# Moving the output-projection partial products of an attention stage behind its last head, and taking three small VectorE steps apart

## What is computed

```python
sc = einsum('bqhcd,bkhcd->bhcqk', qb, kb) * scale        # c = 0, 1
p = softmax(where(causal, sc, NEG_INF))
a = p[:, :, 0] - lam * p[:, :, 1]
outs.append(einsum('bhqk,bkhe->bqhe', a, vb))
...
o = rms_norm(o, sub_norm) * (1.0 - lam_init)
x = x + o.reshape(b, s, N_HEADS * V_DIM) @ w_o
```

## Time and profile before

| | before |
|---|---|
| median of 3 runs | 1104.06 us |
| profiled execution | 1104.02 us, span 1102.2 us |
| TensorE busy | 1092.7 us, 99% of the span |
| VectorE busy | 785.6 us, 71% |
| ScalarE busy | 479.7 us, 44% |
| granted TensorE clock | 1.000 |

### The profile page before, as it was taken

The page is one execution under the profiler, slowest core; times in us unless marked ns, Lnnn a source line. Parts: engine busy times, 40 slices in busy tenths (PEclk is TensorE's granted clock), DMA queues, the critical chain, the costliest instruction groups (busy, mean ns, idle before and its releaser), DMA issues.

```text
span 1102.2 us, 13435 instructions
## 1 busy us (share of the span) xinstructions
PE 1092.7 (99%) x5168; PEld 901.6 (82%) x5168; DVE 785.6 (71%) x980; ACT 479.7 (44%) x695; POOL 77.3 (7%) x58
## 2 busy tenths in 40 slices
PE   8999999999999999999999999999999999999998
PEld 7888888888888888888888877778888888888887
DVE  4765554787787787788764488966678688678686
ACT  7221234354353353354632367845444344344442
POOL 0000012000000000001430122103000000000000
PEclk9999999999999999999999999999999999999999
DMA  7433463314415315301232201072313414314202
GB/s 191 101 92 101 139 204 96 112 42 156 113 39 170 98 38 172 96 1 39 96 115 96 95 24 36 2 230 77 96 58 129 120 58 141 108 58 151 79 0 77
DMA packets 144752, 105.90 MB, mean 96 GB/s; under 512 B 12592, under 2 KB 121136, under 8 KB 144688
## 3 DMA queue, kind: packets, MB, share of 16 engines
q1 hardware_dynamic: 143648, 105.03, 31.3%
q10 hardware_dynamic: 1040, 0.00, 0.1%
HBM read 102.93 MB, written 2.10 MB: 95 GB/s over the span
## 4 chain that ended last, share of the span: by engine, by line
PE 95%; DVE 2%; issue 1%; ACT 1%; DMA 1%; SPq 0%; ACTq 0%; DVEq 0%
PE ps L601 32%; PE ps L628 28%; PE ps L488 19%; PE ps L690 10%; PE ps L715 2%; PE ps L754 1%; PE ps L777 1%; DMA kv<-in_x 1%; PE ps L766 1%; DVE nmax L1563 1%; ACT kv L1110 0%; PE ps L570 0%; PE ps L583 0%; PE ps L664 0%; PE ps L757 0%
## 5 line engine op out<-in xcount | busy, mean ns | idle before, releaser
L601 PE MATMUL ps<-h,w_hi 128*128 128x512 f32 x1024 | 316.1, 390 | 0.0
L628 PE MATMUL ps<-w_hi,h 128*128 128x512 f32 x896 | 277.4, 389 | 0.0
L601 PEld LDWEIGHTS ps<-h,w_hi 128*128 128x128 f32 x1024 | 191.6, 188 | 39.3
L601 PE MATMUL ps<-h,w_lo 128*128 128x512 f32 x512 | 199.3, 389 | 0.0
L628 PEld LDWEIGHTS ps<-w_hi,h 128*128 128x128 f32 x896 | 168.2, 188 | 34.7
L488 PE MATMUL ps<-h,w_hi 128*128 128x512 f32 x608 | 187.9, 390 | 0.2 <-DVE w_lo L1238 0.2
L628 PE MATMUL ps<-w_lo,h 128*128 128x512 f32 x448 | 174.3, 389 | 0.0
L967 ACT ACTIVATE w_hi<-b_raw 128x1024 fp32r<-128x1024 f32 x80 | 82.0, 1054 | 141.5 <-PE ps L601 81.9
L488 PEld LDWEIGHTS ps<-h,w_hi 128*128 128x128 f32 x608 | 113.7, 188 | 23.8 <-DVE w_lo L1238 0.4
L488 PE MATMUL ps<-h,w_lo 128*128 128x512 f32 x304 | 118.3, 389 | 0.0
L1300 DVE TENSOR_TENSOR w_lo<-b_raw,w_hi 128x1024 fp32r<-128x1024 f32 x80 | 95.9, 1223 | 26.4 <-ACT w_hi L967 26.4
(11 more groups left out here) (136 smaller groups left out, 1203.6 us busy)
## 6 DMA issues: line engine op xcount, KB each, us to landing
b_raw<-in_w_down SPq DMA_DIRECT2D x64, 512.0 KB, 4.5
w_raw<-in_w_up SPq DMA_DIRECT2D x64, 512.0 KB, 4.0
w_raw<-in_a_w_in SPq DMA_DIRECT2D x23, 512.0 KB, 3.7
w_raw<-in_w_kv SPq DMA_DIRECT2D x16, 512.0 KB, 3.7
w_raw<-in_a_w_out SPq DMA_DIRECT2D x8, 512.0 KB, 4.1
w_raw<-in_w_q SPq DMA_DIRECT2D x8, 512.0 KB, 3.5
w_raw<-in_w_o SPq DMA_DIRECT2D x8, 512.0 KB, 4.4
kv<-in_x SPq DMA_DIRECT2D x4, 512.0 KB, 6.6
```

The costliest lines, as they stand in the source:

```text
L601: last = nc.tensor.matmul(ps[:, v % 4, :], w[:, s_, k * P:(k + 1) * P], h_of[inp][:, half, k, :], start=(k == 0 and i == 0), stop=(k == KC ...
L628: last = nc.tensor.matmul(ps[:, CHAIN[p][tb], :], op[half][:, k, tb * P:(tb + 1) * P], w[:, s_, cols], start=(FRESH[p] and k == 0 and i == ...
```

## The change

On TensorE all units leave the steps: the heads run without them, and behind `weights_T` of the last step stand three units of block 0, `values(31)`, three more of block 0, then six each of blocks 1 and 2, then block 3 as before. The splits of slabs 2 and 3 leave head 7's steps: on VectorE both stand behind the last join, on ScalarE one stands ahead of `out_hi(6)` and one behind the last `evacuate`.

On VectorE `weights` becomes three functions, and `out_sums` loses its epsilon term to a function of its own. In every head other instructions now stand between a reciprocal, its factor and its join. Two new semaphores count the factors and the epsilon terms. No instruction is added or taken away.

```diff
-WO_FILL = {(3, 1): (0,), (3, 2): (1,), (4, 1): (2,), (5, 1): (3,), (6, 1): (4,), (7, 1): (5,)}
-WO_EARLY = {1: (0,), 2: (1,), 7: (2, 3)}
+WO_EARLY = {1: (0,), 2: (1,)}
...
-                if h == 3:
-                    pe.wait_ge(s_qsq, 16)
-                if h >= 3:
-                    project_out(0, WO_FILL[h, 1])
                 weights_T(n + 1)
...
-                if h == 3:
-                    project_out(0, WO_FILL[h, 2])
-                if h == H - 1:
-                    pe.wait_ge(s_exp, 2 * STEPS - 2)
-                    project_out(1, range(0, 3))
                 values(n)
                 values(n + 1)
...
-                if h == H - 1:
-                    project_out(1, range(3, 5))
...
+            pe.wait_ge(s_qsq, 16)
+            project_out(0, range(0, 3))
+            values(STEPS - 1)
+            project_out(0, range(3, 6))
             pe.wait_ge(s_exp, 2 * STEPS)
-            project_out(1, range(5, 6))
-            project_out(2, range(0, 2))
-            values(STEPS - 1)
-            project_out(2, range(2, 6))
+            project_out(1, range(0, 6))
+            project_out(2, range(0, 6))
...
+                if h == H - 1:
+                    split(S_WO + 2)
                 if h:
                     out_hi(h - 1)
                 evacuate(n + 3)
+            split(S_WO + 3)
...
+            def reciprocal(m):
+                h, i = divmod(m, 4)
+                dve.wait_ge(s_exp, 2 * m + 1)
+                V.reciprocal(rinv[:, m % 2, 0:1], rsum[:, h % 2, i, 1:2]).then_inc(s_sc, 1)
+
+            def factor(m):
+                dve.wait_ge(s_sc, m + 1)
+                dve.wait_ge(s_exp, 2 * m + 2)
...
+            def join(m):
+                dve.wait_ge(s_sf, m + 1)
...
+            def out_eps(h):
+                if h:
+                    dve.wait_ge(s_oms, h)
+                dve.wait_ge(s_exp, 8 * h + 8)
...
                 row_max(n + 2)
-                weights(n + 1)
+                reciprocal(n + 1)
+                if h:
+                    out_eps(h - 1)
+                factor(n + 1)
                 if h < 4:
                     q_norm_part(4 + h)
+                join(n + 1)
...
                 row_max(n + 3)
+                reciprocal(n + 2)
                 if h:
                     out_ms(h - 1)
-                weights(n + 2)
+                factor(n + 2)
+                join(n + 2)
                 if h < H - 1:
                     row_max(n + 4)
+                reciprocal(n + 3)
                 if h:
                     out_norm(h - 1)
                 if h < 4:
                     q_lo(4 + h)
-                weights(n + 3)
+                factor(n + 3)
+                if h < H - 1:
+                    reciprocal(n + 4)
+                join(n + 3)
                 if h < 3:
                     q_stats(5 + h)
                 if h < H - 1:
+                    factor(n + 4)
                     row_max(n + 5)
-                    weights(n + 4)
+                    join(n + 4)
+            split(S_WO + 2)
+            split(S_WO + 3)
+            out_eps(H - 1)
```

More of the change, by code:

```diff
@@ L266, in build @@
         s_sc = sem("s_sc")
+        s_sf = sem("s_sf")
         s_at = sem("s_at")
@@ L273, in build @@
         s_ost = sem("s_ost")
+        s_oep = sem("s_oep")
         s_oms = sem("s_oms")
@@ L1563, in row_max @@
                 V.tensor_reduce(nmax[:, b, :], ps[:, 2 * b:2 * b + 2, 0:kw], AX_X, ALU.max, negate=True).then_inc(s_mx, 1)
-            def weights(m):
+            def reciprocal(m):
[3 more added lines that the diff above has]
+            def factor(m):
                 h, i = divmod(m, 4)
                 b = m % 2
[L1569 to L1572, removed]
+                dve.wait_ge(s_sc, m + 1)
                 dve.wait_ge(s_exp, 2 * m + 2)
                 V.scalar_tensor_tensor(rinv[:, b, 1:2], rinv[:, b, 0:1], lams[:, 5:6], rsum[:, h % 2, i, 0:1],
-                                       ALU.mult, ALU.mult).then_inc(s_sc, 1)
-                dve.wait_ge(s_sc, 2 * m + 2)
+                                       ALU.mult, ALU.mult).then_inc(s_sf, 1)
+            def join(m):
+                b = m % 2
+                kw = (m % 4 + 1) * P
+                dve.wait_ge(s_sf, m + 1)
                 if m >= 2:
@@ L1585, in out_sums @@
                 V.tensor_reduce(osum[:], o_sq.rearrange("p (t e) -> p t e", t=TB), AX_X, ALU.add).then_inc(s_ost, 1)
+            def out_eps(h):
+                if h:
+                    dve.wait_ge(s_oms, h)
+                dve.wait_ge(s_exp, 8 * h + 8)
                 V.scalar_tensor_tensor(oeps[:], rsum[:, h % 2, :, 0], EPS, rsum[:, h % 2, :, 0],
-                                       ALU.mult, ALU.mult).then_inc(s_ost, 1)
+                                       ALU.mult, ALU.mult).then_inc(s_oep, 1)
             def out_ms(h):
-                dve.wait_ge(s_ost, 2 * h + 2)
+                dve.wait_ge(s_ost, h + 1)
+                dve.wait_ge(s_oep, h + 1)
                 if h:
@@ L1623, in _ @@
             row_max(1)
-            weights(0)
+            reciprocal(0)
+            factor(0)
+            join(0)
             q_lo(3)
```

## The result

The changed kernel takes 1107.18 us (median of 8 runs) against 1103.97 us for the kernel before (8 runs): a ratio of 1.003 with a 95% interval of 1.0021 to 1.0038, 3.2 us slower. The profiled execution took 1107.16 us with a span of 1105.4 us, 3.2 more than the span before.

A forecast was written before the change was run, and what follows sets the result against it. A dependence loop through VectorE and TensorE, without the unit, was taken to bound heads 4 to 6. Head terms 0.88 + 0.40 + 0.57 + 0.59 + 0.82 = +3.26 us gave 1107.3 us, range 1105.6 to 1108.5.

The forecast's parts named there:

- head 3 was to gain 0.48: Head 3: earlier first join, epsilon term and factor on VectorE save 0.48 us; two units paid with 1.36, net +0.88.
- heads 4 to 6 were to gain 0.28, 0.11 and 0.09: Heads 4 to 6: shorter by these us, each paying 0.68 for its moved unit: net +0.40, +0.57 and +0.59.
- head 7 was to gain 3.26: Head 7: without splits and units 8.13 us in place of 11.39; six moved units cost 4.08, net +0.82.
- The unit's 0.68: Behind the steps: each moved output-projection unit costs 0.68 us with nothing hiding it; 11 units add 7.5 us.
- the loop: Heads 4 to 6: dependences from third-step scores through VectorE and TensorE to the next head's; 8.62 us, 8.51 after.
- The second route: Scores behind the third transpose also wait for fourth-step exponentials, 2.76 us after its row maximum; 0.03 us of gain lost.
- Rival 1: VectorE's own queue sets the head's length: heads 4 to 6 take 8.04 us; +1.7, 1105.7 us; chance 0.12.
- Rival 2: Split steps on VectorE give nothing, only moved units count: loop stays 8.62 us; +4.2, 1108.3 us; chance 0.08.
- Rival 3: In TensorE's in-order queue the unit delays later transpose and scores, so removing it gains: -2.3, 1101.7 us; chance 0.05.
- The costs that no row of before showed: VectorE instructions when nothing waits for them: 0.07 us taken for the reciprocal, 0.14 for the factor.
- Rival 4: TensorE's clock falls because it idles more often: one head's matmuls cost some 4 us more, 1111 us; chance 0.03.
- DMA: Loads of slabs 4 and 5 start some 4 to 6 us later, behind the moved splits; counted at nothing.

## Why the prediction was right

It said 1107.3 us; measured are 1107.18. The sum held by its terms, and not by errors that cancel: head 3 was to gain 0.48 and gained 0.52; heads 4 to 6 were to gain 0.28, 0.11 and 0.09 and gained 0.31, 0.12 and 0.11; head 7 was to gain 3.26 and gained 3.29. The unit's 0.68 held too: five put back gave 3.42. In head 7, built up from head 5's rows, the steps themselves came as said: out_norm 5.83 us after the scores (said 5.85), the output transpose at 6.58 (6.59), the last transpose at 7.74 (7.77).

- *What bounds the heads.* The prediction leans on the loop's sum coming out at 8.62, the head's length. That shows nothing by itself: start-to-start times along any route from one head's scores to the next one's add up to the head. What made it the loop is that no handover on it has slack: the scores' mask is followed by the row maximum after 0.32 us before and after the change, and the join by the transpose after 0.05. The experiments show it: an instruction costs 0.13 us a head on the loop and 0.00 off it, a unit 0.61 and 0.00.
- *The second route.* The scores behind the third transpose were to be held by the fourth step's exponentials, 2.76 us after its row maximum (703.34). They start at 706.09, 2.75 after it, 0.06 behind the end of this row:

```profile
705.83 0.20 ACT L1102 ACTIVATION_READ_ACCUMULATOR kv<-ps,nmax 128x1 f32 x1
```

- *Rival 1 (VectorE is the bound)* falls: heads 4 to 6 took 8.48 to 8.50 and not 8.04. The page "Perfetto Trace Analysis" of the Trainium skill, section "Identifying the Most-Contended Engine", would have had VectorE improved first. The trace shows it 97% busy before, and that only 0.1 of the 0.56 us saved there reached the head's length.
- *Rival 2 (the order gives nothing)* falls: it is worth 1.0 to 1.1 us in both kernels. The Trainium skill's page "VectorE: DVE Perf Modes", section "The DRAIN you can't avoid", says that the next instruction doesn't start until the pipe is empty, but also that one which isn't held starts earlier; the prediction weighed the first sentence alone. The rows fit the second: a reciprocal costs 0.07 us with an independent instruction behind it and 0.18 or 0.19 with its factor behind it.
- *Rival 3 (a unit holds up the steps)* falls by the five units back.
- *The costs that no row of before showed.* The reciprocal cost 0.07 as taken; the factor 0.13 (706.44 to 706.57) against 0.14.
- *Expected and not quite met.* By the trace TensorE idles 0.67 us in each of heads 4 to 6, where about 0.9 was said, and 1.74 in head 7, where 2.1 was. The difference is the way of counting: a bracket starts at the end of the last row, the forecast at the start where a next one would have come. The two transposes at 702.97 held TensorE for 0.31 us before, and the six value matmuls 0.74; now the next rows come after 0.86 and 1.08 us (702.97 to 703.83, 704.50 to 705.58), 0.89 more. VectorE is busy 8.02 us in head 5, against 7.9.
- *Rival 4 (the clock)* was rated 0.03 with a price of 4 us, for which the prediction gives no rows. A fall of the clock does happen in kernels near this one: it cost 1.2 us where its trace shows it, with the splits back in head 7, and the changed kernel had one run in eight that was 1.7 us longer at a lower mean clock. The argument against it was too light: it looked at the longest wait alone (1.11 us), and with two units in head 7 the clock fell behind waits of 0.66, 0.30 and 1.24 us.
- *DMA.* Nothing was counted, and nothing came: the loads of slabs 4 and 5 start at 725.88 us in place of 722.02, and ScalarE's split of slab 5 waited 2.41 us for its transfer, but TensorE runs on through its units without a wait meanwhile.

## What to carry to other kernels

When two engines are both over 95% busy, follow the suspected loop on both timelines and look at each handover: the receiver must start as soon as the giver is done, by the same short step every time. The sum around it comes out at the period on any route, so it is no test. Put one small instruction on the loop and the same one off it; if only the first lengthens the period, the loop is found, and every edit can be priced by whether it lies on it. Work put between dependent steps is free only in the waits that the loop leaves; moved out of them it is paid in full, and moved behind the next transpose it was paid nearly in full as well.

## What the runs showed of the hardware that I had not expected

- TensorE's granted clock fell to 0.50 for about 3.2 us behind waits of 0.67, 1.69 and 1.23 us, though a single wait of 1.11 us had left it at 1.00. With two units in these waits the mean clock was below 1.000 in two runs of four, with three in none of five.
- A `tensor_scalar` of 128x128 from SBUF costs VectorE 0.13 us start to start, where joins of 128x128 cost 0.27 (700.88 to 701.15 in the kernel before).
